# A two-block transformer on one core: the mixing of the first block in another order, with four tiles open at once

## The reference, cut to what matters

```python
h = rms_norm(x, norm1)
lru_x, lru_g, q, k, v, g, z = split(h @ w_in)
lru_x = causal_depthwise_conv(lru_x, conv_w, conv_b)
lru_o = rg_lru(lru_x, lru_wa, lru_ba, lru_wi, lru_bi, lru_lambda) * gelu(lru_g)
    # r, i = sigmoid(block_diag(lru_x)); a = exp(-8 * r * softplus(-lambda))
    # h_t = a_t * h_{t-1} + sqrt(1 - a^2) * i * x_t
log_alpha = log_sigmoid(z @ gla_w_alpha + gla_b_alpha) / 16
o = gla_chunk_causal(q * 64**-0.5, k, v, log_alpha)      # 8 chunks of 64 tokens, 4 heads
gla_o = rms_norm(o, gla_norm) * silu(g)
x = x + concat([lru_o, gla_o]) @ w_out
h = rms_norm(x, norm2)
x = x + (silu(gate) * up) @ w_ffn_out                    # gate, up = split(h @ w_ffn_in)
```

## Time and profile before

| what | us |
|---|---|
| median of 3 runs (2135.0 to 2136.17) | 2135.5 |
| the profiled execution: its time | 2137.6 |
| the profiled execution: its span, first to last instruction | 2135.8 |
| TensorE busy | 2081.1 (97%) |
| VectorE busy | 1042.2 (49%) |
| ScalarE busy | 829.5 (39%) |

### The profile page before, as it was taken

One profiled execution on the slowest core, in us unless ns is written; L12 is line 12 of the kernel. 1 busy time (PEld: TensorE's weight loads), 2 busy tenths in 40 slices (PEclk: granted clock), 3 DMA queues, 4 the chain that ended last, 5 costly groups with the idle time before them and its releaser, 6 DMA issues.

```text
span 2135.8 us, 26857 instructions
## 1 busy us (share of the span) xinstructions
PE 2081.1 (97%) x10760; PEld 1735.9 (81%) x10760; DVE 1042.2 (49%) x1806; ACT 829.5 (39%) x1361; POOL 14.3 (1%) x28
## 2 busy tenths in 40 slices
PE   7899999999999999999999999999899999999998
PEld 5678788888887887878988888898788789888887
DVE  4645454443443452533654442268677746444323
ACT  4563333323323233333433322345577744332222
POOL 0000000000000000000000000000000000000000
PEclk9999999999999999999999999999899999999999
DMA  4212232333331322322232323333011022322332
GB/s 136 69 60 79 79 103 95 98 97 94 97 106 56 103 70 74 96 72 93 75 100 99 99 88 97 111 143 129 31 41 41 2 94 75 99 99 99 92 96 70
DMA packets 52971, 184.50 MB, mean 86 GB/s; under 512 B 5946, under 2 KB 8266, under 8 KB 52592
## 3 DMA queue, kind: packets, MB, share of 16 engines
q1 hardware_dynamic: 50400, 171.99, 24.9%
q0 software_dynamic: 2160, 10.63, 1.5%
q10 hardware_dynamic: 288, 0.17, 0.0%
HBM read 180.62 MB, written 2.14 MB: 86 GB/s over the span
## 4 chain that ended last, share of the span: by engine, by line
PE 89%; DVE 6%; ACT 3%; issue 1%; DMA 0%; SPq 0%; DVEq 0%; ACTq 0%
PE bank L449 66%; PE bank L597 6%; PE bank L469 6%; PE bank L975 2%; PE bank L839 1%; DVE WL L1531 1%; PE bank L957 1%; PE bank L829 1%; PE bank L942 1%; PE bank L943 1%; ACT WH L1031 1%; PE bank L648 0%; DMA RAW<-in_w_in_t 0%; PE bank L731 0%; DVE XT L1916 0%
## 5 line engine op out<-in xcount | busy, mean ns | idle before, releaser
L1531 DVE TENSOR_TENSOR WL<-RAW,WH 128x1024 fp32r<-128x1024 f32 (+1 forms) x326 | 391.2, 1204 | 547.9 <-ACT WH L1031 547.2
L449 PE MATMUL bank<-AH,WH 128*128 128x512 f32 x1488 | 588.4, 398 | 16.8 <-ACT AH L1041 9.2
L449 PE MATMUL bank<-AL,WH 128*128 128x512 f32 x1488 | 581.6, 394 | 1.0 <-DVE AL L1549 1.0
L449 PE MATMUL bank<-AH,WL 128*128 128x512 f32 x1488 | 580.5, 394 | 1.9 <-DVE WL L1531 1.9
L1031 ACT ACTIVATE WH<-RAW 128x1024 fp32r<-128x1024 f32 (+1 forms) x326 | 337.7, 1041 | 571.2 <-PE bank L449 468.4
L449 PEld LDWEIGHTS bank<-AH,WH 128*128 128x128 f32 x1488 | 282.9, 191 | 79.0 <-issue 13.0
L449 PEld LDWEIGHTS bank<-AH,WL 128*128 128x128 f32 x1488 | 283.1, 190 | 62.6 <-DVE WL L1531 2.8
L449 PEld LDWEIGHTS bank<-AL,WH 128*128 128x128 f32 x1488 | 283.1, 191 | 59.2 <-DVE AL L1549 2.0
L449 PE MATMUL bank<-HH,WH 128*128 128x512 f32 x484 | 188.3, 389 | 0.0
L449 PE MATMUL bank<-HLO,WH 128*128 128x512 f32 x484 | 188.3, 389 | 0.0
L449 PE MATMUL bank<-HH,WL 128*128 128x512 f32 x484 | 188.3, 389 | 0.0
(11 more groups left out here) (352 smaller groups left out, 2742.9 us busy)
## 6 DMA issues: line engine op xcount, KB each, us to landing
RAW<-in_ffn_in SPq DMA_DIRECT2D x132, 512.0 KB, 3.5
RAW<-in_ffn_out SPq DMA_DIRECT2D x48, 512.0 KB, 3.5
RAW<-in_ret_t SPq DMA_DIRECT2D x32, 512.0 KB, 3.6
RAW<-in_ffn_out SPq DMA_DIRECT2D x24, 384.0 KB, 3.1
RAW<-in_w_in_t SPq DMA_DIRECT2D x17, 512.0 KB, 3.9
RAW<-in_ret_v SPq DMA_DIRECT2D x16, 512.0 KB, 3.7
RAW<-in_ret_out SPq DMA_DIRECT2D x16, 512.0 KB, 3.6
RAW<-in_nsa_t SPq DMA_DIRECT2D x9, 512.0 KB, 3.5
```

Source lines behind the costliest of these rows:

```text
L449: t = e.matmul(BANK[b][:, :], wt[:, sl], xx[:, slot(kk) if name == "nsa_out" else kk, :], start=kk == 0 and n == 0, stop=kk == kt - 1 and ...
L1531: e.tensor_tensor(WL[w][:, 0:n], RAW[r][:, 0:n], WH[w][:, 0:n], ALU.subtract).then_inc(w_low.did(v))
```

## The change

It does the following in the first block's mixing.

- The first four tiles (0, 1, 16, 10) are all open while the slices come, each one slice behind the tile before (`first_opening`). Their weights come in halves of 256 KB between the slices, straight into places of their own (FIRST over VG and SG), and their high and low parts lie in MH and ML. GpSimd's loads of the block-diagonal weights wait for the last slice.
- The squares are added up on VectorE (ACC); one group of row sums stands behind the first matmul of tile 11, the spreading behind its ninth (`first_scales`). Tile 11 has bank 4.
- Tile 8 has the gate's logits in its middle. The gate pair f uses banks 6 and 7 or 4 and 5 by turns, the pair for f = 3 comes directly behind the pair for f = 2, ahead of tile 12. GLA's steps stand one tile earlier.
- ScalarE and VectorE work by pairs (alpha, gates, decays, roots of f = 0 and 1, then 2 and 3), and with `ahead` at written places.
- Units of w_out 1 and 2 have places over LB, that of ffn1_in 2 the place over T. ffn1_in's tiles 4 and 5 take banks 6 and 4, so that later tiles have banks turned by one.

```diff
-        aside = [self.first[name, 0] for name in ("ffn2_in", "kv_t", "ffn3_in")]
+        aside = {self.first[q]: w for q, w in ASIDE.items()}
         for u in range(len(self.units)):
-            w = W_SLOTS if u in aside else turn
...
+            if u < 4:
+                w = W_SLOTS + 1 + u
+            elif u in aside:
+                w = aside[u]
+            else:
+                w, turn = turn, (turn + 1) % W_SLOTS
...
+ASIDE = {("w_out", 1): W_SLOTS + 5, ("w_out", 2): W_SLOTS + 6, ("ffn1_in", 2): W_SLOTS, ("ffn2_in", 0): W_SLOTS,
+         ("kv_t", 0): W_SLOTS, ("ffn3_in", 0): W_SLOTS}
...
-        p.tile("w_in_t", m)
+        p.tile("w_in_t", m, bank=4 if m == 11 else None)
...
-            p.tile(f"ffn{n}_in", m, bank=None if n == 1 else {4: 6, 5: 4}.get(m))
+            p.tile(f"ffn{n}_in", m, bank={4: 6, 5: 4}.get(m))
...
+            slice_of_x(0)
+            first_weights(0, 0)
+            slice_of_x(1)
+            first_weights(1, 0)
+            first_weights(2, 0)
+            slice_of_x(2)
+            first_weights(3, 0)
...
+            first_weights(3, 1)
+            slice_of_x(7)
...
-            def three_skewed(name, ms, x, ready, after):
-                for kk, n in sorted(((kk, n) for kk in range(8) for n in range(3)),
-                                    key=lambda q: (q[0] + 2 * q[1], q)):
-                    part(name, ms[n], kk, x, ready if n == 0 else None)
+            def first_opening(ready):
+
+                for kk, n in sorted(((kk, n) for kk in range(8) for n in range(4)), key=lambda q: (q[0] + q[1], q[1])):
+                    part("w_in_t", OPEN_IN[n], kk, A, ready if n == 0 else None)
+
+            def first_scales():
+
+                for n, (q, kk) in enumerate((q, kk) for q in range(3) for kk in range(8)):
+                    part("w_in_t", 11, kk, A, passes=(q,))
                     if n == 0:
-                        after(kk)
+                        enter(5, ("sums", "a"))
+                        e.wait_ge(*set_v.at("ones"))
+                        e.wait_ge(*added.at(("a", 7)))
+                        for tt in range(4):
+                            t = e.matmul(BANK[5][:, tt:tt + 1], ACC[:, ROWS[tt]], ones[:, :], start=True, stop=True)
+                        t.then_inc(matmul.did(("sums", "a")))
+                    if n == 8:
+                        spread("a", rstok)
...
-            tile("w_in_t", 11, A)
+            for kk in range(8):
+                part("w_in_t", 8, kk, A)
+                if kk == 3:
+                    e.wait_ge(s_bd, 80)
+                    alphas()
             lru_gates(0)
-            tile("w_in_t", 8, A)
...
+            turned_keys()
             tokens("w_in_v", 0, A)
             lru_gates(2)
+            lru_gates(3)
...
             tile("w_in_t", 12, A)
-            lru_gates(3)
+            gla_update()
             tile("w_in_t", 13, A)
-            gla_update()
+            gla_out(0)
             tile("w_in_t", 14, A)
-            gla_out(0)
-            tile("w_in_t", 15, A)
             gla_sums(0)
             gla_out(1)
+            tile("w_in_t", 15, A)
+            gla_sums(1)
             tile("w_in_t", 4, A)
...
+            alpha(0)
+            alpha(1)
+            ahead(7)
+            alpha_exp(0)
+            alpha_exp(1)
+            alpha_log(0)
+            alpha_log(1)
+            ahead(8)
+            lru_gates(0)
+            lru_gates(1)
+            ahead(9)
+            lru_decay(0)
+            lru_decay(1)
+            key_scales(0)
+            key_scales(1)
+            ahead(10)
+            lru_root(0)
+            lru_root(1)
+            turned_keys(0)
+            turned_keys(1)
+            ahead(14)
...
             for d in (15, 13, 11, 9, 7, 5, 3, 1):
+                if d == 9:
+                    invert("a", rstok, 4, free_a.at(("sums", "a")))
                 after_lambda(d + 2)
...
+            ahead(5)
+            stream_scales()
+            lru_evac(0)
+            gate_rows()
+            ahead(6)
+            lru_evac(1)
+            qk_evac(2)
+            lru_conv(0)
+            ahead(7)
+            lru_conv(1)
...
+            scaled_keys(0)
+            scaled_keys(1)
+            lru_evac(3)
+            lru_scan(0)
             lru_scan(1)
+            ahead(10)
             lru_conv(2)
-            before("w_in_t", 3)
-            lru_evac(3)
             lru_conv(3)
-            before_tokens("w_in_v", 0)
-            lru_decay(2)
+            ahead(14)
```

More of the change, by code:

```diff
@@ L208, in build @@
             XP = [sb(f"XP{i}", [128, S + 3], stack=ar) for i in range(2)]
-            LB = [[sb(f"LB{i}_{j}", [128, S], stack=ar) for j in range(5)] for i in range(2)]
+            with ExitStack() as over:
+                LB = [[sb(f"LB{i}_{j}", [128, S], stack=over) for j in range(5)] for i in range(2)]
+            W_OUT = [sb(f"W_OUT{i}", [128, 1024], F32R, ar) for i in range(4)]
+            sb("behind", [128, 1024], stack=ar)
             HL = sb("HL", [128, 4, S], stack=ar)
@@ L324, in build @@
         H = [slice(256 * h, 256 * h + 256) for h in range(2)]
+        HALF = [slice(512 * h, 512 * h + 512) for h in range(2)]
         ORDER = (0, 3, 1, 2)
@@ L686, in tensor_program @@
[L686 to L693 removed]
+                y, b = LB[f % 2][0], 4 + 2 * ((f + 1) % 2)
+                enter(b, ("lru_a", f))
+                e.wait_ge(*lru_v.at(("conv", f)))
@@ L1118, in lru_root, with alpha @@
                 e.activation(tt[:, :], r[:, :], ACT.Sqrt).then_inc(lru_a.did(("root", f)))
-            before("w_in_t", 11)
-            lru_gates(0)
-            before("w_in_t", 8)
-            for f in range(2):
+            def alpha(f):
                 e.wait_ge(*matmul.at(("zf", f)))
@@ L1142, in scalar_program, with turned_keys @@
                 e.activation(EG[:, f, :], EG[:, f, :], ACT.Exp, scale=1.0 / 16).then_inc(gla_a.did(("kexp", f)))
-            before("w_in_t", 2)
-            lru_decay(1)
-            lru_root(1)
-            before("w_in_t", 3)
-            for f in range(2):
+            def turned_keys(f):
                 e.wait_ge(*matmul.at(("kt", f)))
@@ L1226, in scalar_program @@
                 if f > 2:
-                    before("w_out", f)
+                    ahead(p.first["w_out", f] + LOOK + f // 7)
                 e.wait_ge(*free_v.at(("w_out", f)))
```

346 lines of the change are left out of this document (201 added, 145 removed).

## The result

The changed kernel takes **2102.5 us** (median; 2102.1 to 2104.6 in four runs) where the kernel before takes 2135.8 beside it: a ratio of 0.9844, 95% interval 0.9827 to 0.9861. It gained 33.3 us. The profiled execution took 2104.6, with a span of 2102.8.

The account below looks back on a forecast made before the run. TensorE was taken as the bound, busy 2081.1 of 2135.8 us. Terms 9.5 + 8.5 + 7.6 - 1.0 + 1.3 + 6.1 = 32.0 off 2135.5 give 2103.5, stated as 2104; own range 2098 to 2111 (62%).

Parts of the forecast that it names:

- Opening: Start to tile 11's end: four open tiles stop TensorE waiting for slices early, ending at about 40.9; gain 9.5 us.
- Loads behind waits: ScalarE's first slice and the sums' root: table loads of 1.28 us stand behind waits; first matmul 0.9 us later.
- 12 matmuls per slice: Opening: each slice releases up to 12 matmuls, 5.1 or 2.7 us against 1.8 per slice, so waits end at about 10.4.
- Tiles 8 to 3: Tile 11's end to the values, by alpha in tile 8 and ScalarE's pairs: 29.2 us instead of 37.7; gain 8.5.
- new wait for XP: Before tile 8: TensorE waits for VectorE's copy of tile 0 out of its bank, 0.9 us.
- margin of 0.6 for KG: Before the transposes: VectorE has the scaled keys ready 0.6 us before TensorE asks.
- Values and gates: 96 matmuls and one gate pair in 23.5 us instead of 31.1, thin cover at third unit's low weights; gain 7.6.
- first rival: VectorE becomes the bound between 36 and 92 us; up to 11.4 us lost, so 2115; 16% for 2111 to 2121.
- GLA: GLA, tiles 12 to 7: same work, low clock left in place, gain 0, minus 1.0 us allowed for two thin places.
- second rival: Clock at GLA goes another way: 4.5 us, so 2099 staying high, 2108 falling twice; 12% for high, 2091 to 2098.
- w_out: w_out: places over LB remove waits for weights of tiles 1 and 2, not all of 2.2 us; gain 1.3.
- ffn1: ffn1_in to tile 4: the third tile's own place removes the wait and low clock, 23.4 us for 29.6; gain 6.1.

Follow-up runs that it names:

- run 1: Changed kernel with two one-column ScalarE activations that load the tables ahead of the waits for constants and sums; 2098.6 us.
- run 4: Changed kernel with three tiles open one slice apart instead of four, tile 10 whole behind them; 2099.9 us.
- run 5: Changed kernel with three tiles open two slices apart instead of four one slice apart, tile 10 whole behind them; 2102.0 us.
- Run 6: Changed kernel with the four first weights in whole pieces of 512 KB, converted whole instead of in halves; 2104.5 us.
- Run 3: Changed kernel with ScalarE's pairs undone: alpha, gates and decays one channel tile after the other; 2107.7 us.
- run 7: Changed kernel with three extra VectorE additions ahead of the low weights of the values' third unit; 2102.5 us.
- run 8: Changed kernel unaltered again, 2103.3 us; with gla_out(1) moved to the middle of tile 15, 2100.9; with short and long matmuls mixed at GLA, 2108.9.
- Run 2: Changed kernel without the own place of ffn1_in's third tile and the extra unit converted ahead; 2106.5 us.
- run 10: Changed kernel with two early table loads, twelve matmuls before the first slice and gla_out(1) in the middle of tile 15; 2095.6 us.

## Why the prediction was right

**The sum held because its terms nearly did**, not by two large errors that cancel: the largest miss of a term is 1.3 us of 32, and some of the small misses cancel. But the terms were sized better than they were explained, above all that of the opening.

**Opening (9.5, measured 10.35).** Right in its place and nearly in size, partly for another reason than I gave and partly by luck: with the sums at 31.59 or 33.12, where other profiles of the same opening have them, it would have measured 11.3 or 9.8. Loads behind waits: right, shown by run 1. There the Trainium skill (ScalarE: Activation LUTs, What ACT_TABLE_LOAD costs) has 2.66 us with a drain; the rows above show 1.28 and the user 0.01 behind it. I let small gaps delay the clock to 15.3; TensorE had none, and it rose at 12.54, 3.9 us behind the first matmul, in the other six profiles at 11.1 to 14.3. I held the 12 matmuls per slice to be what ends the waits; runs 4 and 5 show that three tiles, even two slices apart, wait no more than four. Run 6 gives 1.2 to 2.7 us to the halves. One group of sums in place of four is an estimate from the two traces (0.81 us between long matmuls, before 1.71 and three times 0.81): 3.3. And before, TensorE waited for tile 0's bank inside this stretch:

```profile
44.82 0.50 PE L449 MATMUL bank<-AH,WH 128*128 128x512 f32 x1 [1.22 <-DVE XP L1589]
```

Against these stands the first matmul, 0.7 later. What remains is some 4 to 5 us. That it comes from VectorE's and ScalarE's work on squares, which no longer waits for the groups of sums, is only argued: no run puts them back.

**Tiles 8 to 3 (8.5, measured 8.94).** The new wait for XP came, with 0.44 instead of 0.9, and the transposes waited for nothing. Run 3 shows ScalarE's pairs as the cause of 3.4 us; alpha inside tile 8 and the new places in VectorE's list are argued. My margin of 0.6 for KG was right as a row (scaled keys end 0.7 before the transposes), but too small as a price: ScalarE had 2.4 us to give.

**Values and gates (7.6, measured 7.04).** Without the wait before the transposes the values run at the higher pace. The third unit's low weights were 0.3 us late, as feared (80.60, where its turn was at 80.30); run 7 shows a cover of nothing. So the first rival's mechanism is real, one step away: each microsecond more on VectorE here is one on the path.

**GLA (-1.0, measured 0.06).** Here the step itself was wrong: I took 1.0 off for state updates and weights, and neither made TensorE wait. The low clock that I left in place was left in size, not in place. By the rows of this stretch at the higher pace (3.32 us for gla_out, 5.60 for a tile) it cost 4.8 us before, all in gla_out(1) and the tile behind it, and 4.7 now: 1.6 behind gla_out(0) (the tile from 111.11 on starts 0.43 apart) and 3.2 from gla_out(1) on, which takes 4.91 instead of some 5.6. So the second rival's price for the clock, 4.5, was right, and run 8 took 4.6 of it away by moving one call, which I had not seen. Its other half, a second fall for another 4.5, did not come with the fall at gla_out(0).

**w_out (1.3, measured 1.70) and ffn1 (6.1, measured 4.78).** Waits and low clock are gone. For w_out no run takes the places over LB back, so that cause is argued. The 1.3 too much at ffn1 is a mis-sized term (its working, 29.6 less 23.4, even gives 6.2): I put 0.8 for f1's row sums (those of the stream behind w_out), taking the group of eight of the first stream; they have sixteen short matmuls, 1.70 us, and long matmuls stand 0.231 apart there, not 0.227. Run 2 shows the place as the cause of 2.6 of the 4.78.

## What to carry to other kernels

Look for a table load whose instruction also waits: the load stood behind the wait here, and one small activation of the same kind ahead of it took 1.29 and 1.06 us off the path. When TensorE has no wait left, look at its rows of short matmuls: the granted clock fell there, and parting two such rows by half a tile was worth 4.6 us there and about 2 of the whole time, while mixing short with long cost more than it saved. Where the clock may fall or not, compare stretches between marks in the trace; the whole time moved by 0.8 to 6 us between executions of one kernel and hid a wait of 2.

## What was not expected of the hardware

**Untouched code differs by the clock.** From ffn1's spreading matmuls to the end the thirteen profiles take 1874.5 to 1880.4 us, though no edit changes the work there. The changed kernel's takes 1878.8 and run 4's 1875.5, with the same list of waits to 0.1 us. Windows of 460 us from that mark, the first of the changed kernel, the second of run 4:

```profile
224.04:684.04 460.00, 458.35 (x2029) 376.95 (x2028) 210.01 (x264) 144.21 (x178) 2.72 (x5) 0.99 0.32 94
```

```profile
220.56:680.56 460.00, 458.35 (x2044) 377.03 (x2043) 211.60 (x265) 144.22 (x178) 2.73 (x5) 1.00 0.31 95
```

Fifteen more matmuls in the same time, 3.4 us at 0.227, though only the opening was changed. In run 8's kernel with gla_out(1) moved it went the other way, 1880.4: of 4.6 us won at GLA, 2.7 reached the span (2099.8, against 2102.5 in the second profile of the changed kernel). The move alone does not decide that: run 10 has it too, and takes 1877.3.

**The two paces.** Before its first slice TensorE idles 8 us, and then 7 to 14 matmuls run 0.43 apart in the seven profiles; after 24 short ones that keep it busy from 1.52 on, none does. Behind the wait of 2.67 in run 3 the clock fell, behind those of 1.95 in run 7 and 1.73 in run 2 it did not; but in the kernel before it fell behind one of 1.74, the same place as run 2's. So the length of a wait alone does not tell which way it goes.
